# One projection item per slot, prompt attention in 37 slots from the 35th, and weights and bias rows asked for from ACT's queue

## The reference, cut to what matters

```python
q, k, v, fz = columns of rms_norm(x) @ w_in           # 8 heads of 64 each
logf = log_sigmoid(fz + b_forget)
# prompt: causal, a bias from the cumulative sum d of logf
p = softmax(q @ k.T / 8 + d[t] - d[s]);  out = p @ v    # 1024 x 1024 per head
# samples: the same over 4096 cached tokens (32 pages of 128) and the 4 new ones
p = softmax([q @ k_past.T / 8 + bias, q @ k_new.T / 8 + bias]);  out = p @ [v_past, v_new]
```

## Time and profile before

| | us |
|---|---|
| median of 3 runs | 2040.56 (2038.02 to 2043.32) |
| the profiled execution | 2035.48 |
| its span, first to last instruction | 2033.8 |
| slots 0 to 9 | 70.60 to 149.09 |
| slots 10 to 28 | 149.09 to 272.87 |
| slots 29 to 72 | 272.87 to 545.81 |

### The profile page before, as it was taken

One profiled execution on the slowest core, in us unless ns is written; L12 is line 12 of the kernel. 1 busy time (PEld: TensorE's weight loads), 2 busy tenths in 40 slices (PEclk: granted clock), 3 DMA queues, 4 the chain that ended last, 5 costly groups with the idle time before them and its releaser, 6 DMA issues.

```text
span 2033.8 us, 33501 instructions
## 1 busy us (share of the span) xinstructions
PE 1876.1 (92%) x12402; PEld 1109.1 (55%) x12402; DVE 832.8 (41%) x1867; ACT 442.9 (22%) x1021; POOL 250.4 (12%) x381
## 2 busy tenths in 40 slices
PE   6999988888999999999999898994999999999994
PEld 4677655545588868888864466543333333333331
DVE  5644477777666423333354406334111111111115
ACT  3111133434301011011111205231222222212213
POOL 0203233323100000000000000000111111111120
PEclk9999999989999999999999999997999999999997
DMA  7759999999912130210111204444999999999966
GB/s 269 260 168 348 351 355 360 357 323 344 318 51 87 46 127 11 63 52 11 63 65 63 85 1 156 145 148 174 353 382 386 378 370 375 374 371 376 368 225 261
DMA packets 208164, 458.56 MB, mean 225 GB/s; under 512 B 18722, under 2 KB 47419, under 8 KB 207619
## 3 DMA queue, kind: packets, MB, share of 16 engines
q1 hardware_dynamic: 177554, 365.30, 50.1%
q0 software_dynamic: 30448, 91.13, 12.6%
HBM read 432.44 MB, written 32.17 MB: 228 GB/s over the span
## 4 chain that ended last, share of the span: by engine, by line
PE 79%; DVE 6%; DMA 4%; issue 4%; ACT 4%; DVEq 2%; SPq 1%; POOLq 0%; POOL 0%; ACTq 0%
PE ps L1322 16%; PE ps L1632 11%; PE ps L1663 6%; PE ps L1151 6%; PE ps L1387 6%; PE ps L1643 5%; PE ps L1416 5%; PE ps L1672 3%; PE ps L1123 3%; PE ps L1166 3%; PE ps L1505 2%; PE ps L1274 2%; DMA kraw<-in_cache_k 2%; PE ps L1254 2%; DMA vpage<-in_cache_v 2%
## 5 line engine op out<-in xcount | busy, mean ns | idle before, releaser
L1632 PE MATMUL ps<-gu,xgT 128*64 128x512 f32 x1024 | 226.8, 595 | 0.9 <-ACT xgT L1983 0.9
L2166 DVE STREAM_TRANSPOSE kt<-kraw 128x1024 f32<-128x1024 f32 x128 | 151.2, 1219 | 47.1 <-DMA kraw<-in_cache_k 37.8
L1322 PE MATMUL ps<-xnT,ring 128*128 128x264 f32 x672 | 159.1, 387 | 0.6 <-DMA xnT<-xn_d 0.6
L861 POOL DMA_DIRECT2D vpage<-in_cache_v x228 | 122.8, 539 | 293.2 <-PE ps L1274 236.3
L2904 DVE TENSOR_TENSOR sig_a<-ps,sig_a 128x256 f32<-128x256 f32 x32 | 13.6, 425 | 324.6 <-ACT sig_a L1987 324.6
L1632 PEld LDWEIGHTS ps<-gu,xgT 128*64 128x64 f32 x1024 | 70.7, 137 | 131.9 <-issue 128.7
L1322 PEld LDWEIGHTS ps<-xnT,ring 128*128 128x128 f32 x672 | 127.3, 190 | 23.8 <-DMA xnT<-xn_d 1.8
L1663 PE MATMUL ps<-wd,hidT_a 128*64 128x512 f32 x512 | 118.6, 605 | 19.1 <-ACT hidT_a L1993 10.5
L1643 PE MATMUL ps<-gu,xgT 128*32 128x512 f32 x1024 | 115.8, 592 | 0.0
L1151 PE MATMUL ps<-xnT,early 128*128 128x352 f32 x320 | 101.1, 472 | 4.5 <-DVE xnT L2110 4.5
L1151 PEld LDWEIGHTS ps<-xnT,early 128*128 128x128 f32 x320 | 60.6, 194 | 38.3 <-issue 8.7
(11 more groups left out here) (446 smaller groups left out, 2907.6 us busy)
## 6 DMA issues: line engine op xcount, KB each, us to landing
kraw<-in_cache_k SPq DMA_DIRECT2D x256, 256.0 KB, 5.0
wd<-in_w_expert_down SPq DMA_DIRECT2D x31, 2048.0 KB, 21.0
gu<-in_w_expert_gate SPq DMA_DIRECT2D x30, 2048.0 KB, 20.4
gu<-in_w_expert_up SPq DMA_DIRECT2D x30, 2048.0 KB, 25.0
vpage<-in_cache_v POOLq DMA_DIRECT2D x228, 256.0 KB, 5.5
ring<-in_w_in SPq DMA_DIRECT2D x12, 1024.0 KB, 8.0
yy<-y_d SPq DMA_DIRECT2D x16, 512.0 KB, 9.9
early<-in_w_in SPq DMA_DIRECT2D x6, 1024.0 KB, 11.5
```

The costliest lines, as they stand in the source:

```text
L861: eng.dma_start(vpage[value_place(n)][:, p, :], t["cache_v"][ds(page, 1)].rearrange("a s d -> (a s) d")).then_inc(v_in[value_place(n)], 16)
L1322: last = nc.tensor.matmul(bank(R.bank(name, f, q))[:, 0:QT], weight[:, k], src[:, k, cols], start=k == 0, stop=k == HK - 1)
L1632: last = nc.tensor.matmul(bank(0)[h * BA:(h + 1) * BA, :].rearrange("p (x n) -> p x n", x=2), src[:, k, 0:BA], weight[:, k, :, h * DE // 2 ...
L2166: last = nc.vector.transpose(kt[n % 2].rearrange("p c e s -> p (c e s)")[:, x * 1024:(x + 1) * 1024], kraw[n % 2].rearrange("p c d -> p (c ...
```

## The change

One item goes to each of slots 0 to 33. The order of the items changes in one place: the v item of the sample tokens' second column half comes sixth among the v items, in slot 13, before the pages' weighing needs it in slot 17. The halves of the prompt attention are spread over slots 35 to 71, 37 slots instead of 43, and k's output rows over slots 36 to 44. The new tokens' scores move from slot 5 to slot 6. SP no longer asks for v's and k's weights and for the bias rows: ACT does, right behind the copy that shows that the place is free (`load_behind`, and after the turned probabilities of halves (7, 0) and (15, 0) for the third and fourth pair of rows).

```diff
-        ITEMS = ([("q", f, n) for f, n in REST] + [("v", half, i) for half in range(2) for i in VTILES]
+        ITEMS = ([("q", f, n) for f, n in REST] + [("v", 0, i) for i in VTILES[:5]] + [("v", 1, PT)]
+                 + [("v", 0, i) for i in VTILES[5:]] + [("v", 1, i) for i in VTILES[1:]]
                  + [("k", f, n) for f, n in REST])
-        PROMPT0, PROMPT_SLOTS, KOUT0 = 29, 43, 30
+        PROMPT0, PROMPT_SLOTS, KOUT0 = 35, 37, 36
         def items(n):
-            first = n + min((n + 1) // 2, 6)
-            return ITEMS[first:first + (2 if n < 12 and n % 2 == 0 else 1)]
+            return ITEMS[n:n + 1]
...
-            if n == 5:
+            if n == 6:
                 R.add("dve", "snew", banks=TURNS)
...
-                if n == 7:
-                    R.made(sp, "q", 1, 1)
-                    early_load(0, O_V)
...
-                if n == 35:
-                    R.made(sp, "k", 3, 1)
-                    sp.wait_ge(xn_stored, 16)
-                    load_negk(1)
...
+            def load_weights(slot, c0):
+                act.dma_start(early[slot], w3(t["w_in"], c0 + slot * 256, 256)).then_inc(early_in[slot], 16)
+            def load_negk(hp):
+                for p in range(2):
+                    act.dma_start(negk[hp % 2][p], neg_d[2 * hp + p:2 * hp + p + 1, 0:SEQ].to_broadcast([P, SEQ])
+                                  ).then_inc(negk_in[hp % 2][p], 16)
+            def load_behind(kind, a, b):
+                if (kind, a, b) in (("q", 1, 1), ("q", 3, 1)):
+                    load_weights(a // 2, O_V)
+                if kind == "v" and b == PT - 1:
+                    load_weights(a, O_K)
+                if (kind, a, b) == ("k", 1, 1):
+                    act.wait_ge(neg_stored, 16)
+                    load_negk(0)
+                if (kind, a, b) == ("k", 3, 1):
+                    act.wait_ge(xn_stored, 16)
+                    load_negk(1)
...
+                    if p == 0 and k in (PT - 1, 2 * PT - 1):
+                        load_negk(k // PT + 2)
                 for item in items(n):
                     copy_item(*item)
+                    load_behind(*item)
```

More of the change, by code:

```diff
@@ L926, in load_rev @@
                              .unsqueeze(1).to_broadcast([4 * H, DS, SU * PAGE])).then_inc(rev_in[b % 2], 16)
[L928 to L939, removed]
             load_unit(0), load_unit(1)
```

## The result

The changed kernel takes 2052.53 us (median of 16 runs, 2041.32 to 2056.34) beside 2038.58 us for the kernel before on the same chip (16 runs, 2033.02 to 2044.19): ratio 1.0062, 95% interval 1.0049 to 1.0075. It is slower by 14 us (13.95 by the medians, 12.6 by the ratio), where 4 us faster was forecast, and its median lies outside the forecast range. The profiled execution took 2054.27 us, its span 2051.3.

What follows compares the result with a forecast made beforehand. PE's work and the softmax chain were taken to bound the slots, DMA only partly. -15.9 + 33.6 - 13.0 + 1 - 10 = -4.3 us, from the median 2040.56 to 2036.3; range 2024 to 2050 (8 in 10).

Steps and rivals of the forecast that it cites:

- Slots 0 to 9: First ten slots: five v items leave, less about 1.1 to 1.3 us of new PE wait: -15.9 us.
- Slots 10 to 34: Item slots before the prompt stage: 157.4 us in sum, +33.6; PE idling over 5 us in slots 10 to 33 refutes.
- v slots: The 16 slots with a v item from slot 10 on: 96 us, between PE's 93.6 alone and a bound of 104.
- Prompt attention, 251 for the stage: Prompt stage from slot 35 on: takes 251 us, DMA about 0.90, doubles (slots with two halves) near 7.5.
- rival B: Prompt stage: dense doubles leave PE no slot to catch up, total 2046.3 to 2057, stage over 257 us; chance 0.20.
- The -13.0: Prompt attention: slots sorted by their number of halves, 19.2 us less in key slots, 6.2 more in slots 64 to 72.
- The loads: Weight and bias-row loads issued by ACT, partly between probability copies: +1 us, bounds -1 to 9.6.
- PE waiting for ACT behind its issues for over 3 us: Sign that would show the forecast wrong altogether: PE waits over 3 us for ACT behind its DMA issues.
- Relief: Prompt stage: lower DMA share in longer key slots shortens PE's waits and raises its clock: -10 us, bounds 0 and 20.
- Rival A: From slot 10 on DMA bounds, so the early gain counts whole: -15.9 us, total 2024.7; chance 0.25.

Runs made afterwards that it cites:

- e13: Changed kernel with both halves of a unit sharing a slot, all loads on SP, prompt stage over 35 slots: 2045.44 us, 1.0033 of before.
- e7: Changed kernel with only the eight bias rows asked for by SP again, weights still by ACT: 2043.10 us, 1.0018 of before.
- e10: e7 plus eight 8-byte DMAs issued by ACT where the changed kernel asks for its bias rows: 2045.37 us, 1.0028 of before.
- e2: Changed kernel's schedule with all weight and bias-row loads asked for by SP, five slots before their use: 2041.71 us, 1.0014 of before.
- e3: Changed kernel with both halves of a unit always sharing a slot, loads still on ACT, 37 slots: 2034.89 us, 0.9985 of before.
- e5: e3 with all weight and bias-row loads asked for by SP: 2032.07 us, 0.9973 of before.
- e12: e5 with the prompt stage over 33 slots instead of 37: 2035.16 us, 0.9985 of before.
- e16: Changed kernel with a whole unit in each of slots 35 to 64, last two in 66 and 68, loads on ACT: 2031.59 us, 0.9970 of before.
- e4: Changed kernel with every double slot joining one unit's second half with the next unit's first: 2070.87 us, 1.0179 of before.
- e11: Kernel before with only the pairing changed, both halves of a unit in one slot over the same 43 slots: 2045.16 us, 1.0034.
- e14: e13 with weights and bias rows asked for by ACT: 2041.93 us, 1.0014 of before.

## Why the prediction was wrong

*Slots 0 to 9* (-15.9): right within a microsecond. 63.51 us is 15.0 less, DMA at 0.77 for "about 0.8"; PE idles 2.2 us there where 1.1 to 1.3 had been expected.

*Slots 10 to 34* (157.4): right, 157.12. The v slots took 95.3 for the 96 chosen between two close limits, of which PE was busy 94.1, and over the whole stretch PE idled 3.0 us, under the 5 that would have refuted it. The Trainium skill's HBM limit of about 358 GB/s per core (DMA: Bandwidth & Descriptors, "Where 436 GB/s comes from"), by which the v slots were to take 99.7, was not tested by them: at 359 GB/s they moved 34.2 MB in 95.3 us, less than the 35.7 that the estimate had put there. It does not bind as such in this kernel: 375 GB/s held over 41 us, and a slot of e13 ran at 402. So slot 35 started at 291.35, forecast 290.5.

*Prompt attention, 251 for the stage*: wrong, 266.75, past the 257 that the prediction had named as the sign of rival B. Two terms failed. (The -13.0 was to be confirmed by a plain count, "worth 15"; the count that stands there gives 13.7.)

*"The loads", +1, bounds -1 to 9.6*: the mis-sized term. Only ACT's issue time was priced. The runs give some 9 us for the bias rows (e7 against the changed kernel), at the edge of the upper bound, but not for the bound's reason: e10 leaves about 3 to the issue. The rest goes with late keys (DVE's wait for them 12.4 us for 5.4): the same bytes asked for from a third queue arrive, by the likely reading, beside the keys and not behind them. The text had excluded that by saying that "SP's and POOL's order is otherwise the same"; the order is, the landing times are not. The sign named for it, PE waiting for ACT behind its issues for over 3 us, was looking at the wrong engine.

*"Relief", -10*: did not come in the changed kernel. DMA's share fell further than forecast, to 0.86 for 0.90, the direct waits for values vanished, and yet PE idled as long and the clock was worse. The step that failed is that a lower mean share of DMA would shorten PE's waits and raise its clock: an average share was taken for slack. DVE waited longer for keys at a share of 0.86 (12.4 us) than at 0.96 (11.2), and most of it in two places. Loads have to land within the slot or two that their places allow, and a mean says nothing of that: in e13 DMA stands at 1.04 in the gap and at 0.69 three slots on. With all loads on SP's queue (e2) the stage came out at 252.45 with a clock of 0.97, near the number forecast, and yet the total was +4: the slots before it took 3 us more than in the changed kernel, its stage ended at 546.01 (before 545.81), and PE's wait for the diagonals was still 13.0 us. The rest of the difference between its trace and that of the kernel before, 5.3 us, lies behind the stage, in the part that varies between two lengths for a reason not found.

The loss against the kernel before needs both things together, mixed doubles and loads on ACT. With mixed doubles the ratio is 1.0062 with the loads on ACT and 1.0014 on SP; with whole units in the same 37 slots it is 0.9985 (e3) and 0.9973 (e5). e3, which keeps the change whole but for the pairing, comes out at -2.8, near the -4.3 forecast; as the forecast knew nothing of the pairing, that nearness proves none of its terms.

*Rival B* named the sign and nearly the place: PE waits for DVE's diagonals. But it called that "a wait that a data load has no part in", and slot 54 shows a late key load ahead of the longest of them. Its mechanism, doubles so dense that PE can't catch up, is refuted: e12 and e16 are denser, a whole unit in every slot, and faster. What hurts is a double whose halves are of two units (e4, +33) and, less surely, a slot without any: e13 and e11 lose with such slots, but e5 gains with three of them in the key part. The forecast's method, sorting slots by the number of halves, put both kinds of double under one mean of 7.89. Sorting them by kind would not have helped: in the kernel before they took 7.87 and 7.94, and only in the changed kernel, where up to three doubles follow each other, 9.82 and 7.76. What could have been read beforehand is the order of DVE's work, with a wait for keys ahead of diagonals that PE needs in the same slot.

*Rival A* (DMA bounds, the early gain counts in full) did not happen either, though e12's end, 17 us on value pages with PE busy for 6, looks like its beginning once the attention is out of the way.

## What to carry to other kernels

Before a load is moved to another engine's queue, ask what it will land beside: on its old queue it waited behind the loads already asked for, on a new one it may take bandwidth from them at once. Whether that costs depended here on the schedule around it (0.48% with mixed doubles, nothing that shows with whole units), so look for what stands behind the consumer's wait in its list. And where an evenly spread loop is respread, look at which pieces now meet in one step and which steps are empty: here, with the same work, that was worth more (36 us of the total between e3 and e4) than everything that the change moved on purpose.

## What had not been expected of the hardware

Beside 512 KB rows asked for by ACT, 256 KB key loads took a median of 9.7 and 11.0 us to land, where the stage's is 5.4; in e16 it was 8.3 and 6.9. With one 7 us wait of PE, slot 54 had a granted clock of 0.68, and eight matmuls of line 1237 took 1.66 us for 1.07 before the wait. And a slot without attention could be nearly as long as one with a unit: slot 46 took 5.64 us in e13, with DMA at 1.04, for 6.13 in e12; but in e14 it took 3.20, with DMA at 0.68, and in e11 such slots took 2.0 to 3.6.
